# Two transformer blocks in float32 on one core: an mLSTM recurrence laid out by token, gates and convolutions moved into their linears, long convolutions merged

## The reference

```python
def mlstm_mixer(xn, w_in, conv_w, conv_b, gate_b, head_norm, w_out):
    proj = xn @ w_in                      # 3088 columns: q,k 1024 | v 1024 | o 1024 | gates 16
    qk = silu(causal_conv4(proj[..., :1024], conv_w) + conv_b)
    gates = 15 * tanh((g_pre + gate_b) / 15)
    i_pre, log_f = gates[..., :8], log_sigmoid(gates[..., 8:])
    # per head, B = cumsum(log_f), over tokens s <= t:
    #   w[t,s] = exp(B[t] - B[s] + i[s] - m[t]) * (q[t] . k[s]) / 8
    #   h[t] = sum_s w[t,s] v[s] / max(|sum_s w[t,s]|, exp(-m[t]))
    h = rmsnorm(h, head_norm)             # per head, 128 numbers
    return (sigmoid(o_pre) * h) @ w_out

# Hyena, per layer: 1536 columns, a convolution over 3 tokens, split in 3 x 512; then for o in (0, 1):
#   z = (long_conv(z, filter[o]) + skip[o] * z) * gate[o]
# The filters (forward and backward) come from a small sine network times a window and are divided
# by the sum of their absolute values. Long convolutions are products in a spectrum of 256 lines.
```

## Time and profile before

| what | value |
|---|---|
| median of 3 runs | 3400.32 us (3399.54 to 3415.02) |
| profiled execution, device time | 3400.13 us |
| its span, first to last instruction | 3398.3 us |
| mean granted TensorE clock | 0.913 |
| busy: PE, DVE, ACT, POOL | 2941.6, 2106.3, 1482.0, 40.0 us |

### The profile page before, as it was taken

How to read it: one execution, slowest core, us unless ns; L and a number is a source line. 1 busy time by engine, 2 the same in 40 slices (tenths; PEclk the granted TensorE clock), 3 DMA queues, 4 the chain that set the end, 5 groups by cost and what they waited for, 6 DMA issues and landing times. The chain is left out here.

```text
span 3398.3 us, 44680 instructions
## 1 busy us (share of the span) xinstructions
PE 2941.6 (87%) x18175; PEld 2619.8 (77%) x18175; DVE 2106.3 (62%) x2152; ACT 1482.0 (44%) x1353; POOL 40.0 (1%) x65
## 2 busy tenths in 40 slices
PE   5999974699999999999967696898999686899899
PEld 4799973578888888888843584898899584899898
DVE  5555557378888888888846453555555454555554
ACT  3443432156766776676622023343434023343432
POOL 0000000000000000000000000000000000000000
PEclk8899986689999999999979886899999886899999
DMA  5255520089999999999941240344355230354352
GB/s 164 73 178 184 161 88 1 0 300 347 363 333 347 363 333 344 365 333 342 367 135 75 64 124 13 121 165 132 104 185 164 75 113 25 112 161 137 100 186 100
DMA packets 364966, 618.36 MB, mean 182 GB/s; under 512 B 16670, under 2 KB 201092, under 8 KB 363536
## 3 DMA queue, kind: packets, MB, share of 16 engines
q1 hardware_dynamic: 363656, 610.87, 52.3%
q10 hardware_dynamic: 1162, 5.36, 0.4%
HBM read 610.94 MB, written 5.24 MB: 181 GB/s over the span
## 5 line engine op out<-in xcount | busy, mean ns | idle before, releaser
L345 DVE TENSOR_TENSOR slots_low<-slots,w_hi 128x2048 fp32r<-128x2048 f32 (+2 forms) x241 | 542.1, 2253 | 579.7 <-ACT w_hi L334 579.7
L334 ACT ACTIVATE w_hi<-slots 128x2048 fp32r<-128x2048 f32 (+2 forms) x241 | 451.7, 1878 | 585.0 <-PE ps L426 263.1
L1166 DVE TENSOR_TENSOR slots_low<-slots,w_hi 128x2048 fp32r<-128x2048 f32 x224 | 504.0, 2285 | 70.7 <-ACT w_hi L1118 70.7
L426 PE MATMUL ps<-x_hi,w_hi 128*128 128x256 f32 x1488 | 438.3, 295 | 120.1 <-DVE x_lo L497 40.1
L426 PE MATMUL ps<-x_lo,w_hi 128*128 128x256 f32 x1488 | 432.9, 291 | 0.0
L426 PE MATMUL ps<-x_hi,slots_low 128*128 128x256 f32 x1488 | 432.4, 291 | 0.0
L1118 ACT ACTIVATE w_hi<-slots 128x2048 fp32r<-128x2048 f32 x224 | 415.8, 1908 | 1.1 <-DMA slots<-in_moe_w_up_dram 1.0
L426 PEld LDWEIGHTS ps<-x_hi,w_hi 128*128 128x128 f32 x1488 | 298.2, 200 | 126.5 <-issue 89.9
L1050 PE MATMUL ps<-slots_low,x_hi 128*128 128x512 f32 x896 | 349.6, 390 | 0.0
L426 PEld LDWEIGHTS ps<-x_lo,w_hi 128*128 128x128 f32 x1488 | 298.4, 201 | 0.5
L426 PEld LDWEIGHTS ps<-x_hi,slots_low 128*128 128x128 f32 x1488 | 297.8, 200 | 0.0
(11 more groups left out here) (517 smaller groups left out, 5782.9 us busy)
## 6 DMA issues: line engine op xcount, KB each, us to landing
slots<-in_moe_w_gate_dram SPq DMA_DIRECT2D x112, 1024.0 KB, 5.1
slots<-in_moe_w_up_dram SPq DMA_DIRECT2D x112, 1024.0 KB, 5.2
slots<-in_moe_w_down_dram SPq DMA_DIRECT2D x112, 1024.0 KB, 4.9
slots<-in_mlp_w_dram SPq DMA_DIRECT2D x64, 1024.0 KB, 5.3
slots<-in_w_in_dram SPq DMA_DIRECT2D x54, 1024.0 KB, 5.3
slots<-in_ffn_w_gate_dram SPq DMA_DIRECT2D x14, 1024.0 KB, 5.0
slots<-in_ffn_w_up_dram SPq DMA_DIRECT2D x14, 1024.0 KB, 5.0
slots<-in_ffn_w_down_dram SPq DMA_DIRECT2D x14, 1024.0 KB, 4.9
```

The lines of the kernel that those rows point to most:

```text
L334: act.activation(w_hi[:, s.buffer, 0:s.kt * s.cols], slots[:, s.slot, 0:s.kt * s.cols], ACT.Copy).then_inc(w_hi_done, 1)
L345: dve.tensor_tensor(slots_low[:, s.slot, 0:n], slots[:, s.slot, 0:n], w_hi[:, s.buffer, 0:n].bitcast(F32), ALU.subtract).then_inc(w_lo_don ...
L426: mm = pe.matmul(b[:, t * T:(t + 1) * T], w, xx[:, k, :], **flags)
L1166: dve.tensor_tensor(low[i % NS], raw[i % NS], his[i % R].bitcast(F32), ALU.subtract).then_inc(lo_done, 1)
```

## The change

The constants. `keep_st` (128x128, zeros and ones) becomes `later` (128x256, zero or 1e30), by which a margin is masked before the exponential. The window and the transform are laid out with every second token on a partition, and the spectrum's 256 lines are ordered so that line k and line 255-k stand together: with even and odd tokens apart, one product per half is enough and a sum and a difference join them.

The mLSTM linear. The slab of the gates moves from the thirteenth place to the fifth. The convolution, the transposes of the gates, tanh, exp, ln, the scans, the floors, the spreads of M, the margins and their exponentials become hooks of the linear. The recurrence then has tokens t on partitions: products with a column of ones give the denominator as one number per head and token, the norm takes its squares with an accumulator, and denominator and norm are one number per token (128x16 for all heads); the result is then transposed to features.

```diff
@@ mLSTM: order of the slabs
-        stream.weights(A["mlstm_w_in"][0], 256)
+        for lo, hi in ((0, 1024), (3072, 3088), (1024, 3072)):
+            stream.weights(A["mlstm_w_in"][0][:, lo:hi], 256)
@@ mLSTM: hooks of the linear
+                    def first_tap(s):          # ScalarE, tiles 2s and 2s+1
+                        def f(act, more):
+                            act.wait_ge(cleared, 3)
+                            act.wait_ge(more["emptied"], s + 1)
+                            for k in (2 * s, 2 * s + 1):
+                                act.activation(qk[:, k, :], raw[:, k, 0:T], ACT.Copy, scale=conv_w(0, k)).then_inc(more["tapped"], 1)
+                        return f
...
+                    hooks = {("dve", 0): bias, ("pe", 5): turn_gates, ("dve", 7): scans, ("act", 8): floors, ("pe", 8): spread_half(0), ("dve", 9): margins(0),
+                             ("act", 10): decays(0), ("pe", 10): spread_half(1), ("dve", 11): margins(1), ("act", 12): decays(1)}
+                    hooks["act", 2], hooks["act", 3] = first_tap(0), first_tap(1)
+                    hooks["act", 4], hooks["act", 5] = both(smooth(0), first_tap(2)), both(smooth(1), first_tap(3))
+                    hooks["act", 6], hooks["act", 7] = both(smooth(2), cap_gates), smooth(3)
+                    for s in range(4):
+                        hooks["dve", 3 + s] = other_taps(s)
...
@@ mLSTM: recurrence, TensorE
+                            def mix(h):
+                                pe.wait_ge(weighted, h + 1)
+                                blocks = [(0, gt[:, h, 0:P], 0, True, True), (1, gt[:, h, P:T], 0, True, False), (1, gt[:, h, T:W3], 1, False, True)]
+                                for t, w, kt, first, last in blocks:
+                                    pe.matmul(bank(4)[:, 2 * h + t:2 * h + t + 1], w, ones[:, 0:1], start=first, stop=last)
+                                for t, w, kt, first, last in blocks:
+                                    mm = pe.matmul(mean(h)[:, t, :], w, v[:, kt, h * P:(h + 1) * P], start=first, stop=last)
+                                mm.then_inc(summed, 1)
...
@@ mLSTM: norm on numbers per token (VectorE; the squares and the root are ScalarE's)
+                            dve.wait_ge(squared, NH * TT)
+                            st.did(dve.scalar_tensor_tensor(out=flat(root[:, :, :]), in0=flat(sums[:, :, :]), scalar=1.0 / P, in1=flat(den[:, :, :]),
+                                                            op0=ALU.mult, op1=ALU.add)); st.settle()
+                            dve.wait_ge(rooted, 1)
+                            st.did(dve.reciprocal(flat(root[:, :, :]), flat(root[:, :, :]))); st.settle()
+                            for n in range(NH // 2):
+                                r = root[:, 2 * n:2 * n + 2, :].rearrange("p h t -> p (h t)")
+                                dve.tensor_tensor(hs[:, 2 * n:2 * n + 2].rearrange("p h t n -> p (h t) n"), bank(n).rearrange("p (a n) -> p a n", a=4),
+                                                  r.unsqueeze(2).broadcast_to([P, 4, P]), ALU.mult).then_inc(scaled, 1)
...
```

```diff
+                        def size(i):
+                            dve.wait_ge(mixed, 2 * i + 2)
+                            dve.scalar_tensor_tensor(out=flat(fb[:, 1]), in0=flat(pq[:, 1]), scalar=-1.0, in1=flat(pq[:, 1]),
+                                                     op0=ALU.mult, op1=ALU.max).then_inc(absd, 1)
+                            if i:
+                                dve.wait_ge(summed, i)
+                            dve.wait_ge(absd, 2 * i + 2)
+                            dve.tensor_tensor(flat(ab[:, :, :]), flat(fb[:, 0]), flat(fb[:, 1]), ALU.max).then_inc(added, 1)
...
                         for i in range(N):
-                            scale(i)
+                            size(i)
                             if i + 1 < N:
                                 window(i + 1)
+                            scale(i)
                             store(i)
...
@@ ScalarE
+                            act.wait_ge(mixed, 2 * i + 2)
+                            act.activation(flat(fb[:, 0]), flat(pq[:, 0]), ACT.Abs).then_inc(absd, 1)
+                            act.wait_ge(joined, 4 * i + 4)
                             act.dma_start(spectra_dram[l][o], flat(F[:, :, :])).then_inc(spectra_out, 16)
...
+                            for n, (a, b, op) in enumerate(((2, 3, ALU.add), (3, 2, ALU.subtract), (0, 1, ALU.add), (0, 1, ALU.subtract))):
+                                pool.wait_ge(outed, 4 * i + (3 if n < 2 else 4))
+                                pool.tensor_tensor(F[:, (2, 3, 0, 1)[n], :], halves[:, a, :], halves[:, b, :], op).then_inc(joined, 1)
```

The Hyena branch. The 3-token convolution becomes hooks of its linear (`first_tap` on ScalarE and `other_taps` on VectorE, steps 2 to 6; step 6 has the last two pairs of tiles). The four stages of `hyena` become one, in which the transform, the products, POOL's sums and the back transform are counted part by part:

```diff
+                        for n in (0, 2, 1, 3):
+                            for t in range(TT):
+                                mm = pe.matmul(bank(n), dft[:, t, n // 2, n % 2 * P:(n % 2 + 1) * P], u[:, t, :], start=(t == 0), stop=(t == TT - 1))
+                            mm.then_inc(transformed, 1)
+                        for i, n in enumerate((0, 2, 1, 3)):
+                            pe.wait_ge(product, 4 * o + i + 1)
                             for m in range(4):
-                                for n in range(4):
-                                    mm = pe.matmul(bank(4 + m)[:, 0:T], y[:, n, m * P:(m + 1) * P], idft[:, n // 2, n % 2, :], start=(n == 0), stop=(n == 3))
-                                mm.then_inc(back, 1)
+                                mm = pe.matmul(bank(4 + m)[:, 0:T], y[:, n, m * P:(m + 1) * P], idft[:, n // 2, n % 2, :], start=(i == 0), stop=(i == 3))
+                                if i == 3:
+                                    mm.then_inc(back, 1)
```

More of the change, by code:

```diff
@@ L1521, in hyena @@
             idft = K["idft"][:, :].rearrange("p (s k t) -> p s k t", s=2, k=TT)
-            with ExitStack() as c:
+            slabs = take(2)
+            with ExitStack() as c, stage("turned", "act_out", "dve_out", "transformed", "first", "second", "product", "back", "skipped", "out") as \
+                    (block, turned, act_out, dve_out, transformed, first_, second_, product, back, skipped, outed):
                 u = sb(c, "tokens", [P, TT, 512])
@@ new lines, in layer @@
+                        hooks = {}
+                        for j in range(2, 7):
+                            slabs = (j - 2,) if j < 6 else (4, 5)
+                            hooks["act", j] = first_tap(*slabs)
+                            hooks["dve", j] = other_taps(*slabs)
+                        linear([x], pairs_of(0, [scale_to(hy[:, k:k + 2, 1:T + 1], rs) for k in range(0, 12, 2)]), ("first_tap", "second_tap", "convolved"), pool=pad, hooks=hooks)
+                        x.split = False
@@ new lines, in program, with mean @@
+                    sq = sb(c2, "square", [P, P])
+                    sums, den, root = (sb(c2, n, [P, NH, TT]) for n in ("square_sums", "denominator", "root"))
+                    with stage("scored", "weighted", "summed", "squared", "step", "rooted", "scaled", "turned", "out") as \
+                            (block, scored, weighted, summed, squared, step, rooted, scaled, turned, outed):
+                        def mean(h):
+                            return bank(h // 2)[:, h % 2 * T:(h % 2 + 1) * T].rearrange("p (t n) -> p t n", t=TT)
```

437 lines of the change are left out of this document (250 added, 187 removed).

## The result

The changed kernel takes 3317.85 us (median of 4 runs, 3316.9 to 3319.7), the kernel before, run beside it, 3407.7: ratio 0.973, 95% interval 0.9707 to 0.9753. Forecast were 3275 us, 3258 to 3300. The direction was right. The profiled executions differ by 3398.3 - 3315.1 = 83.2 us of span, two thirds of the 124.9 us that were forecast; the medians differ by 89.8.

The account below looks back on a forecast made before the run. TensorE was taken to bound the mLSTM linear and nearly the spectra; VectorE-led or serial chains bound the rest. Gains of 64.3 (mLSTM), 60.6 (layers) and 0 (spectra), 124.9 us, took 3400.1 to 3275 us, range 3258 to 3300.

Parts of the forecast that it names:

- Low clock at first, as now: mLSTM recurrence: three scores at low clock (3.9 us), five scores (3.3) and eight mixes (10.8) after; 18.0 us in all.
- all at the low clock 31: mLSTM recurrence: the bound of 31 us in place of 18.0 if TensorE's clock stays low throughout.
- rival (2): TensorE's clock does not follow in spectra (+8), recurrence (+13), each hyena (up to 11): +43, 3318 us; chance 0.08.
- changes nothing in the sum of items: mLSTM input linear: moving the gates' slab from last to fifth place costs and gains nothing.
- Spectra, forecast 0: Filter spectra: VectorE becomes the bound and waits for ScalarE; 65.5 us as now, bounds 10 lost to 7 gained.
- The trace so shows hardly a wait on VectorE: Spectra: VectorE's two-input pair took 1.32 us beside POOL, 1.29 with POOL idle, the case against a hold-up by joins.
- Rival (1): Spectra: POOL's joins hold up VectorE, some 3.5 us per unit above the stand: +10, 3285 us; chance 0.12.
- The end of the linear: mLSTM linear: ScalarE's decays and last sigmoid end 5.2 us behind TensorE's last matmul, then 0.5 of barrier.
- the 4 us more that were weighed beside the sum: ScalarE: some 4 us more for three table loads at the skill's 2.66 us per switch; not taken into the sum.
- The tail: mLSTM behind the recurrence: squares, root and reciprocal of 128x16, scalings, outputs and barrier, 10.2 us.
- All three signs of being wrong: Linears over 5 us longer, VectorE's 128x1024 operations over 1.5 us beside POOL, low clock past 5 us of a stage.
- (5): Merged stages still run one behind the other, only barriers and reciprocals go: gain 64 + 20, 3316 us; chance 0.03.

Follow-up runs that it names:

- e16: Changed kernel with each head's keys in a tile of their own, the other 64 rows zero, so scores run over 128 rows: 3304.4 us, ratio 0.9692.
- e2: Changed kernel with the recurrence's denominator products 128 columns of ones wide in place of one: 3303.0 us, ratio 0.9684.
- e1: Kernel before the change with one edit, the gates' slab multiplied fifth in the mLSTM input linear and not last: ratio 1.0004.
- e5: Changed kernel with the four joins of the filter spectra on VectorE behind its stores, nothing on POOL: 3312.3 us, ratio 0.9716.
- e6: Changed kernel with each unit's spectra write issued by POOL behind its joins, not by ScalarE: 3314.6 us, ratio 0.9719.
- e11: Changed kernel with the spectra's joins on VectorE and the sum of sizes ahead of two of three transforms on TensorE: 3307.7 us, ratio 0.9689.
- e10: Changed kernel with the gates' slab columns as stationary side and tokens moving, 256 wide, the gates' four transposes gone: 3310.9 us, ratio 0.9706.
- e9: Changed kernel with the gates' slab widened to 256 moving columns, of which 16 are kept: 3310.4 us, ratio 0.970.
- e7: Changed kernel with POOL's four joins replaced by scaling one of their two tiles by 1.0 (other spectra result): 3316.0 us, one run.

## Why the prediction was wrong

**Recurrence, forecast 18.0, measured 32.8: the main miss.** The step that failed is the clock of the recurrence: "Low clock at first, as now", three scores at the low clock, then five scores and all of "Eight mixes 1.35 = 10.8" at the high one. It took the rise over from the kernel before. There is followed by these two windows, with 64-row scores too, but with mixes whose products move 256 and 128 columns:

```profile
525.00:529.00 4.00, 4.00 (x30) 3.64 (x28) 3.57 (x12) 1.25 (x4) 0.00 (x0) 0.97 0.00 0
529.00:533.00 4.00, 4.00 (x26) 3.67 (x25) 3.58 (x13) 1.22 (x4) 0.00 (x0) 1.00 0.01 4
```

In the changed kernel, with 128 columns and one, the clock stays at 0.50 to the end. The prices of the products were right: its terms for a head, 0.65 and 1.35, doubled and taken eight times, give 32.0. e16 and e2 show the cause as far as an edit can: with keys over 128 rows and all else of the recurrence the same, B is 27.3 where the sum had 28.2. The bound "all at the low clock 31" was written and was the outcome, but rival (2), which holds it, got 0.08, with the gaps of TensorE as its reason; there was no gap.

**The gates' slab, forecast "changes nothing in the sum of items", measured 3.5 alone (e1) and 5.8 to 6.5 in the changed kernel (A 96.84 against 91.1 and 90.4), of which 3.0 are the second fall.** The forecast counts only the work of the items, which the move leaves the same, and not the clock behind a narrow one. The same slab last in the linear had the same low clock behind it, where little on TensorE waited; the earlier trace rows has the linear at 0.99 and the stretch behind it at 0.60, so those rows could not tell whose doing that was.

**Spectra, forecast 0, measured -13.7.** The step that failed is "The trace so shows hardly a wait on VectorE". The earlier trace rows has a POOL operation with 64 elements of one tile; the joins read two tiles of 512. Rival (1) was this, priced at +10 above the stand; e5 and e6 show the turns and the stand as one loss, of 7.1 us where the joins move to VectorE. The other half was no rival: the forecast left out that the sum is queued behind three transforms (the first unit took 18.3 us to its reciprocal where it was 15.3 before, and 16.6 in e11), and TensorE's clock, 0.74 in the middle of the stretch where the earlier trace rows had 0.97. That is the part of rival (2) that names the spectra; its share apart from the order is not shown.

**What held.** The end of the linear: TensorE's last product ends at 495.4, the first score starts at 500.46: 5.1 us where 5.2 + 0.5 were written. Its table loads took 1.28 us each, as the earlier trace rows has it, so the 4 us more that were weighed beside the sum did not come. The tail: 9.8 of 10.2, with the reciprocal of 128x16 at 0.25 us where 13.0 stood. Hooks: at the high clock TensorE's last product ends 85.3 us (e10) and 86.0 us (e9) behind the first split, 85.1 by the sum (481.5 + 4.6 - 401.0). The hyena branch: 74.1 to 44.3, forecast 43.8; the back transform follows the transform without a gap in 7.07 us:

```profile
1877.34 9.63 PE L1572 MATMUL ps<-tokens,dft 128*128 128x512 f32 x16 [0.88 <-DVE tokens L1591]
...
1886.80 7.07 PE L1577 MATMUL ps<-idft,product 128*128 128x256 f32 x32
```

The sum of what was missed: 64.3 - 44.8 = 19.5 in the mLSTM, 13.7 in the spectra, 60.6 - 59.9 = 0.7 in the layers, and 7.8 outside of every stage that was changed (2.6 and 2.0 in the table, 3.2 behind layer 1's branch), together 41.7 = 124.9 - 83.2. The 2.6 and the 2.0 are within the chance of their stretches. The 3.2 are not, and have no experiment. Why the clock of TensorE differs between executions of the same code at the start is open too.

All three signs of being wrong that the prediction named came: TensorE's last product of the mLSTM linear ended 6.6 us later than the sum had it (91.7 us behind the first split), VectorE's 128x1024 operations took 2.0 to 2.3 us beside POOL, and the low clock lasted 32.8 us. That the total lies beside the numbers of rivals (2) and (5), 3318 and 3316, is chance: (2) has up to 22 us lost in the hyena branches, which came within 0.5 us of the forecast in layer 0, and (5) has merged stages that run one part behind the other, which they did not.

The Trainium skill ("TensorE: Matmul & The Clock Gate", What's actually happening) has activity release the throttle and gives the slow state as that of an idle engine. Here TensorE's records were without a gap for 32.8 us and the clock did not rise: where page and measurement differ, the measurement decides. The ends of such records are modelled, so a row of them without a gap is not yet proof of how active the array was.

## What to carry to other kernels

A clock read beside one mix of products doesn't hold for another: when a change narrows the moving side, or halves the rows, price the stage at both clock levels and weigh the lower one by itself, even if TensorE will have no gap; and then try padding, since more columns or rows of zeros can be faster (B 42.65 to 30.5 and to 27.3 here). Put narrow products where little on TensorE follows. Before work goes to POOL, look for VectorE operations with two SBUF inputs beside it and for whoever waits for POOL; a spare engine is the one with free time at that point, which here was TensorE.

## What the runs showed of the hardware that was not expected

- TensorE was 100% busy at 0.50 granted for 32.8 us; the clock reached 1.00 when 64 rows became 128 (e16), or one column became 128 (e2).
- Behind 48 products with 16 moving columns, in a linear at 1.00, the clock fell to 0.50 and was back at 1.00 some 7 us later, with TensorE busy all the time (e1).
- Products with one moving column took 0.48 us each against 0.54 with 128 (three in 1.44 and 1.63 us) at the lower level, 0.24 against 0.30 at the higher one (three in 0.73 and 0.91).
- The scores took 1.22 us over 64 rows and at the lower level, 1.19 over 128 rows (e16, its first); 0.70 and 0.60 at the higher one.
- VectorE with two SBUF inputs beside POOL with two: each operation took 1.7 to 1.8 times as long on VectorE (4.18 us for 2.36) and 1.6 times on POOL (7.87 for 4.92). Beside POOL's scaling with one input (e7) it was 1.2 times on VectorE (2.88 for 2.36) and 1.05 on POOL (6.13 for 5.86).
- A table load on ScalarE took 1.28 us, and the exponential that waited for nothing else started 1.29 us after the load did, at the end of the mLSTM linear as in the earlier trace rows.
